# Expert rows added up in DRAM, the last expert's matrices in halves, and a closing norm by 512 columns

## The reference

```
cl = (xf @ w_coarse) + b_coarse                     # 4 groups, the best one is taken
fl_sel = fine logits of that group's 8 experts      # the best two are taken
gate = p_coarse * softmax of the two fine logits
for grp in range(4):                                # 32 experts in all
    hg = silu(xf @ w_gate[grp]) * (xf @ w_up[grp])  # 2048 -> 512, per expert
    hg = hg * gate
    y = y + hg @ w_down[grp]                        # 512 -> 2048
h = h + y
out = rms_norm(h, final_norm)                       # over 2048 columns
```

## Time and profile before

| | before |
|---|---|
| median of three runs | 1869.32 us |
| profiled execution, own time | 1867.9 us |
| span of its records | 1865.8 us |
| matrices of experts 1 to 31: first issue, last bytes | 898.85 us, about 1831 us |
| last up product, last down product end | 1832.75 us, 1841.51 us |
| last VectorE operation ends | 1863.26 us |

### The profile page before, as it was taken

How to read it: one execution, slowest core, us unless ns; L and a number is a source line. 1 busy time by engine, 2 the same in 40 slices (tenths; PEclk the granted TensorE clock), 3 DMA queues, 4 the chain that set the end, 5 groups by cost and what they waited for, 6 DMA issues and landing times.

```text
span 1865.8 us, 36834 instructions
## 1 busy us (share of the span) xinstructions
PE 1666.8 (89%) x16304; PEld 1183.8 (63%) x16304; DVE 446.4 (24%) x1020; ACT 317.4 (17%) x820; POOL 86.0 (5%) x144
## 2 busy tenths in 40 slices
PE   6999999988988999998999888988898888998894
PEld 5888888867777445575876554654556555565552
DVE  2000333588885201014111100111011100101014
ACT  2112222166665101123000000000000000000001
POOL 1000000000000000001000000000000000000000
PEclk9999999999999999998999999999999999999997
DMA  9932344400000935332799999999999999999995
GB/s 319 181 110 91 116 127 169 180 4 4 4 4 4 339 112 203 124 149 95 300 393 427 428 430 425 423 426 434 420 428 422 427 433 413 435 414 434 419 426 235
DMA packets 95237, 509.75 MB, mean 273 GB/s; under 512 B 39324, under 2 KB 43824, under 8 KB 77088
## 3 DMA queue, kind: packets, MB, share of 16 engines
q1 hardware_dynamic: 87080, 490.27, 65.2%
q0 software_dynamic: 7808, 17.28, 3.0%
q10 hardware_dynamic: 248, 0.65, 0.1%
HBM read 497.66 MB, written 23.10 MB: 279 GB/s over the span
## 4 chain that ended last, share of the span: by engine, by line
PE 70%; DMA 20%; DVE 5%; issue 2%; ACT 1%; SPq 0%; DVEq 0%; POOL 0%; ACTq 0%
PE ps L1909 19%; DMA ring<-in_wu 19%; PE ps L1407 15%; PE ps L1732 6%; PE ps L1897 6%; PE ps L1959 6%; PE ps L1750 1%; PE ps L1801 1%; PE ps L1759 1%; PE ps L1818 1%; PE ps L1621 1%; PE ps L1489 1%; PE ps L1448 1%; PE ps L1470 1%; DMA ring<-y_dram 1%
## 5 line engine op out<-in xcount | busy, mean ns | idle before, releaser
L1909 PE MATMUL ps<-ring,rkv 128*64 128x256 f32 x4096 | 473.7, 392 | 67.2 <-DMA ring<-in_wu 45.8
L1909 PEld LDWEIGHTS ps<-ring,rkv 128*64 128x64 f32 x4096 | 337.5, 141 | 211.5 <-DMA ring<-in_wu 54.5
L1407 PE MATMUL ps<-hnT,ring 128*128 128x256 f32 (+1 forms) x1280 | 282.2, 379 | 2.7 <-ACT hnT L471 1.5
L1407 PEld LDWEIGHTS ps<-hnT,ring 128*128 128x128 f32 (+1 forms) x1280 | 239.1, 187 | 48.2 <-issue 10.1
L1959 PE MATMUL ps<-ring,gg 128*64 128x512 f32 x1024 | 238.0, 619 | 32.1 <-issue 16.1
L1959 PEld LDWEIGHTS ps<-ring,gg 128*64 128x64 f32 x1024 | 84.0, 142 | 164.1 <-issue 145.1
L1318 DVE SCALAR_TENSOR_TENSOR gg<-ps,tmp,gg 128x256 f32<-128x256 f32 x32 | 15.4, 483 | 521.3 <-PE ps L1909 521.3
L1897 PE MATMUL ps<-hnT,sw 128*128 (+1 forms) x1024 | 120.5, 279 | 5.0 <-DVE rkv L1293 2.7
L1897 PEld LDWEIGHTS ps<-hnT,sw 128*128 128x128 f32 x1024 | 117.3, 194 | 11.1 <-issue 8.2
L737 ACT ACTIVATE rkv<-ps 128x512 f32<-128x512 f32 x32 | 19.1, 597 | 547.6 <-PE ps L1959 547.6
L1326 DVE COPY rkv<-ps 128x512 f32<-128x512 f32 x31 | 21.4, 691 | 244.0 <-PE ps L1959 244.0
(11 more groups left out here) (352 smaller groups left out, 1597.7 us busy)
## 6 DMA issues: line engine op xcount, KB each, us to landing
ring<-in_wg SPq DMA_DIRECT2D x32, 4096.0 KB, 19.6
ring<-in_wu SPq DMA_DIRECT2D x32, 4096.0 KB, 21.4
ring<-in_wd SPq DMA_DIRECT2D x32, 4096.0 KB, 17.7
ring<-in_w_in SPq DMA_DIRECT2D x7, 4096.0 KB, 15.3
ring<-in_w_out SPq DMA_DIRECT2D x4, 4096.0 KB, 21.3
ring<-in_w_in SPq DMA_DIRECT2D x16, 512.0 KB, 7.5
y_dram<-tmp POOLq DMA_DIRECT2D x1, 4096.0 KB, 21.3
ring<-in_xatt_wk SPq DMA_DIRECT2D x1, 4096.0 KB, 14.1
```

What stands on the lines that cost most here:

```text
L1407: ins = mm(ps[0:rows_, m % 2, 0:T], lhs, hnT[:, k, :], start=k == 0, stop=k == KD - 1)
L1909: ins = mm(ps[CAP * h:CAP * h + CAP, bank, 0:T], xT[:, k, CAP * i:CAP * i + CAP], slot_k(slot)[:, k, T * h:T * h + T], start=k == 0, stop= ...
```

## The change

1. `y_dram` has 2 rows for each token, and the scatter adds to the stored row (`compute_op=ALU.add`). The tensor is no longer zeroed. After the residual is complete (`xw_add`), SyncE stores it there: four DMAs of 512 KB, 2 MB in all (L347), issued behind the down matrix of expert 0. GpSimd waits for them. One more scatter comes first in each pass, and in the first pass all its rows are out of bounds; the last expert's rows are not scattered at the end.
2. The halves of the columns are laid differently: the two halves `n` of the down product are now columns 0 to 1023 and 1024 to 2047, and in `y_dram` and in `tokA` at the end a row holds 512 columns of each.
3. The last expert's up matrix comes in two DMAs (first and second half of the contraction), its down matrix in four of 1 MB (two column halves by two halves of the contraction). TensorE waits for each half by itself.
4. SyncE reads back 2 MB in four DMAs straight into `tokA`, over the residual, as soon as scatter 30 has landed; it waits for no product. The four wide additions on VectorE are gone.
5. The last eight products are ordered by the tuple `FIN`, each with its own increment of `fin_mm`, and VectorE adds them one by one. The table for the square root is loaded on ScalarE ahead of the squares.
6. Semaphores are merged and renamed (`zeroed`, `rel_in`); this moves no instruction.

```diff
-        c[:, TV + b] = 2 * (np.arange(P) + P * b) - BIG
+        c[:, TV + b] = np.arange(P) + P * b - BIG
...
+        def fin_part(b, h, n):
+            o = D // 2 * h + F * n
+            return tokA[:, b, o:o + F]
-        y_dram = nc.dram_tensor("y_dram", (4 * T, D // 2), F32)
+        y_dram = nc.dram_tensor("y_dram", (2 * T, D // 2), F32)
+        FIN = ((0, 0, 0), (0, 0, 1), (0, 1, 0), (1, 0, 0), (1, 0, 1), (0, 1, 1), (1, 1, 0), (1, 1, 1))
+        FIN_BANK = (0, 1, 2, 3, 6, 7, 4, 5)
...
+            def last_expert(j):
+                sp.wait_ge(S["m_gate"], j + 1)
+                weights(S_GATE, "wg", NE - 1)
+                sp.wait_ge(S["m_up"], j + 1)
+                up = a["wu"][NE - 1].rearrange("(p k) n -> p (k n)", p=P)
+                for h, done in ((0, landed[S_UP]), (1, S["up_rest"])):
+                    q = slice(SLOT // 2 * h, SLOT // 2 * h + SLOT // 2)
+                    sp.dma_start(ring[:, S_UP, q], up[:, q]).then_inc(done, 16)
+                sp.wait_ge(S["m_dn"], 2 * j + 1)
+                down = a["wd"][NE - 1].rearrange("(h p c) n -> p h c n", h=2, p=P)
+                for n, h, done in ((0, 0, landed[S_DOWN]), (0, 1, S["dn_lo"]), (1, 0, S["dn_hi"]), (1, 1, S["dn_hi"])):
+                    q = slice(D // 2 * n, D // 2 * n + D // 2)
+                    sp.dma_start(slot_d(S_DOWN)[:, 2 * h:2 * h + 2, q], down[:, h, :, q]).then_inc(done, 16)
...
+            yv = y_dram.ap().rearrange("(b p h) d -> p b h d", p=P, h=2)
+            sp.wait_ge(S["xw_add"], 8)
+            for b in range(TB):
+                hv = tokA[:, b].rearrange("p (n h c) -> p h n c", n=2, h=2)
+                for h in range(2):
+                    sp.dma_start(yv[:, b, h].rearrange("p (n c) -> p n c", n=2), hv[:, h]).then_inc(S["y_init"], 16)
...
-            with sp.Fori(0, NE - 1) as e:
+            with sp.Fori(0, NE - 2) as e:
                 expert(e + 1, e + 1)
+            last_expert(NE - 1)
...
-            sp.wait_ge(S["m_up"], blocks * NE + 1)
+                    last_expert(b * NE + (NE - 1))
             sp.wait_ge(S["rows_out"], blocks * NE)
-            yv = y_dram.ap().rearrange("(b p r h) d -> p b r (h d)", p=P, r=2, h=2)
             for b in range(TB):
-                sp.dma_start(slot_d(S_UP)[:, 2 * b:2 * b + 2, :], yv[:, b]).then_inc(S[f"y_in{b}"], 16)
-            for b in range(TB):
-                sp.wait_ge(S[f"y_in{b}"], 16)
-            sp.sem_inc(S["last_go"], 1)
+                for h in range(2):
+                    sp.dma_start(tokA[:, b, D // 2 * h:D // 2 * h + D // 2], yv[:, b, h]).then_inc(S[f"y_in{b}{h}"], 16)
...
-                if i == 4:
-                    sp.wait_ge(S["rows_out"], blocks * NE + 1)
+                b, h, n = i // 4, i // 2 % 2, i % 2
+                o = D // 2 * n + F * h
                 sp.wait_ge(S["fin_o"], i + 1)
-                sp.dma_start(ov[:, b, q], tokA[:, b, q]).then_inc(S["out_done"], 16)
+                sp.dma_start(ov[:, b, o:o + F], fin_part(b, h, n)).then_inc(S["out_done"], 16)
...
-            pool.wait_ge(S["pool_step"], 1)
-            pool.dma_start(y_dram.ap().rearrange("(p r) (j n) -> p (r j) n", p=P, n=256),
-                           zeros.unsqueeze(1).broadcast_to([P, 32, 256])).then_inc(S["y_zero"], 16)
...
+            pool.memset(tmp[:, 1600 + NE - 1:1600 + NE], 1.0).then_inc(S["pool_step"], 1)
+            pool.wait_ge(S["pool_step"], 1)
+            pool.wait_ge(S["y_init"], 16 * 2 * TB)
+
+            def scatter(e, c):
                 pool.tensor_copy(sidx[:], rows_of[:, ds(e, 1)]).then_inc(S["sidx_ok"], 1)
-                pool.wait_ge(S["sidx_ok"], j + 2)
-                pool.wait_ge(S["m_ya"], j + 2)
-                pool.wait_ge(S["m_yv"], j + 2)
+                pool.wait_ge(S["sidx_ok"], c + 1)
+                pool.wait_ge(S["m_ya"], c + 1)
+                pool.wait_ge(S["m_yv"], c + 1)
                 pool.sem_inc(S["pool_step"], 1)
                 pool.indirect_dma_start(y_dram.ap(), bass.IndirectOffsetOnAxis(sidx[:, 0:1], 0), ysb, None,
-                                        bounds_check=4 * T - 1, oob_is_err=False).then_inc(S["scattered"], 16)
-                pool.wait_ge(S["scattered"], 16 * j + 16)
+                                        bounds_check=2 * T - 1, oob_is_err=False, compute_op=ALU.add).then_inc(S["scattered"], 16)
+                pool.wait_ge(S["scattered"], 16 * c + 16)
                 pool.sem_inc(S["rows_out"], 1)
...
+                scatter(NE - 1, b * NE)
                 pool.wait_ge(S["r_cnt"], 3 * b + 1)
                 pool.sem_inc(S["pool_step"], 1)
-                scatter(0, b * NE)
-                scatter(1, b * NE + 1)
+                scatter(0, b * NE + 1)
+                scatter(1, b * NE + 2)
                 pool.wait_ge(S["r_cnt"], 3 * b + 3)
                 pool.sem_inc(S["pool_step"], 1)
                 with pool.Fori(2, NE - 1) as e:
-                    scatter(e, b * NE + e)
-                pool.wait_ge(S["last_go"], b + 1)
-                pool.sem_inc(S["pool_step"], 1)
-                scatter(NE - 1, b * NE + (NE - 1))
+                    scatter(e, b * NE + e + 1)
...
-                dc.add(V.tensor_scalar(vals[:, b, :, 0], M2[:, b], cst[:, TV + b:TV + b + 1], None, ALU.add))
+                dc.add(V.tensor_copy(vals[:, b, :, 0], cst[:, TV + b:TV + b + 1].broadcast_to([P, NE])))
...
-            for i in range(8):
+            A(warm, warm, ACT.Sqrt)
+            for i, (n, t, h) in enumerate(FIN):
                 act.wait_ge(S["fin_sq"], i + 1)
-                b, q = i // 4, slice(F * (i % 4), F * (i % 4) + F)
-                A(tokB[:, b, q], tokA[:, b, q], ACT.Square, accum_out=sqp[:, i:i + 1]).then_inc(S["sq_done"], 1)
+                A(tokB[:, t, F * (2 * h + n):F * (2 * h + n) + F], fin_part(t, h, n), ACT.Square,
+                  accum_out=sqp[:, 4 * t + 2 * h + n:4 * t + 2 * h + n + 1]).then_inc(S["sq_done"], 1)
...
-            yy = slot_d(S_UP)
-            for b in range(TB):
-                dve.wait_ge(S[f"y_in{b}"], 16)
-                dc.link(V.tensor_tensor(tokA[:, b, :], tokA[:, b, :], yy[:, 2 * b, :], ALU.add))
-                dc.link(V.tensor_tensor(tokA[:, b, :], tokA[:, b, :], yy[:, 2 * b + 1, :], ALU.add))
-            for i in range(8):
-                b, q = i // 4, slice(F * (i % 4), F * (i % 4) + F)
-                dve.wait_ge(S["fin_mm"], i // 4 + 1)
-                V.tensor_tensor(tokA[:, b, q], tokA[:, b, q], ps[:, i, :], ALU.add).then_inc(S["fin_sq"], 1)
+            def last_rows(i):
+                n, t, h = FIN[i]
+                dve.wait_ge(S[f"y_in{t}{h}"], 16)
+                dve.wait_ge(S["fin_mm"], i + 1)
+                V.tensor_tensor(fin_part(t, h, n), fin_part(t, h, n), ps[:, FIN_BANK[i], :], ALU.add).then_inc(S["fin_sq"], 1)
+            def last_var(t, squares):
+                dve.wait_ge(S["sq_done"], squares)
+                dc.link(V.tensor_reduce(stat(5, 0)[:, t:t + 1], sqp[:, 4 * t:4 * t + 4], AX.X, ALU.add))
+                V.tensor_scalar(stat(5, 1)[:, t:t + 1], stat(5, 0)[:, t:t + 1], 1.0 / D, EPS, ALU.mult, ALU.add).then_inc(S["var_done"], 1)
+            def last_out(t):
+                dve.wait_ge(S["std_done"], 6 + t)
+                dc.link(V.reciprocal(stat(5, 2)[:, t:t + 1], stat(5, 2)[:, t:t + 1]))
+                for h in range(2):
+                    for n in range(2):
+                        o = D // 2 * n + F * h
+                        V.scalar_tensor_tensor(fin_part(t, h, n), fin_part(t, h, n), stat(5, 2)[:, t:t + 1], gain_fin[:, o:o + F],
+                                               ALU.mult, ALU.mult).then_inc(S["fin_o"], 1)
+            for i in range(6):
+                last_rows(i)
+            last_var(0, 14 + 5)
+            last_rows(6)
+            last_rows(7)
-            for b in range(TB):
-                dve.wait_ge(S["sq_done"], 18 + 4 * b)
-                dc.link(V.tensor_reduce(stat(5, 0)[:, b:b + 1], sqp[:, 4 * b:4 * b + 4], AX.X, ALU.add))
-                block_rstd(5, b, 6 + b)
-                for i in range(4):
-                    q = slice(F * i, F * i + F)
-                    V.scalar_tensor_tensor(tokA[:, b, q], tokA[:, b, q], stat(5, 2)[:, b:b + 1], gain_fin[:, q], ALU.mult, ALU.mult).then_inc(S["fin_o"], 1)
+            last_out(0)
+            last_var(1, 14 + 8)
+            last_out(1)
...
+                    if rest is not None and k == KD // 2:
+                        pe.wait_ge(S["up_rest"], rest)
...
                     for n in range(2):
+                        if last and n == 0:
+                            pe.wait_ge(S["dn_lo"], 16 * b + 16)
+                        if last and n == 1:
+                            pe.wait_ge(S["dn_hi"], 32 * b + 32)
...
-                                o = D // 2 * h + F * n
+                                o = D // 2 * n + F * h
...
-            pe.wait_ge(S["m_yv"], blocks * NE + 1)
-            for t in range(TB):
-                for n in range(2):
```

(26 more changed lines are left out.)

35 lines of the change are left out of this document (14 added, 21 removed).

## The result

The changed kernel takes 1874.9 us, the median of 20 runs (1870.72 to 1880.82), and the kernel before 1869.07 us, the median of 20 runs. The ratio is 1.0031, with a 95% interval of 1.0024 to 1.0038: it is slower by about 5.8 us. The prediction said 1874 us. It was the difference of two terms, 13.3 us gained in the tail and 18.6 us lost to scatters that add, and the profile after shows both; "tail" stands here for the time from the issue of the last gate matrix to the end of the span.

A forecast was written before the change was run, and what follows sets the result against it. For half of the time the arrival of 31 experts' matrices by DMA bounds the kernel, then a tail. 1867.9 (profiled) - 13.3 + 18.6 = 1873.2 us, 1874 us for the median; range 1857 to 1889 us.

The forecast's parts named there:

- Tail: End of the kernel: matrices in pieces, earlier read-back and no wide additions were to gain 13.3 us.
- Read-back in time: End of the kernel: 2 MB queue behind the down matrix, landing about 1834 to 1838 us, each part before its addition.
- Small edits: Dropped zeros, stored residual, extra empty scatter, column order and matrix pieces: counted as 0; 5 us without cover for the store.
- The adding scatter: Matrix stream: a second read paid like the first, 0.60 us for each of 31 scatters, 18.6 us lost; chance 0.42.
- The price of 0.60 us for a scatter: Matrix stream: extra time per adding scatter, taken between 0.50 and 0.75 us.
- The rule of the Trainium skill on two source reads: Adding scatters: limited by two source reads on one ring, 1.93 times a copy; the term would be 17 us.
- The swizzle rule: Scatters: four neighbouring partitions share one engine; 0.78 us on the fullest engine, 24 us for the term.
- The share of 2.2% or more: Sign of being right: software queue's share of the DMA engines over 940 to 1790 us, in place of 1.2%.
- Hidden reads: Rival on the adding scatters: second read hidden or nearly, 0 to 4 us, kernel 1856 to 1860 us; chance 0.25.
- Half price: Rival on the adding scatters: second read spread evenly or partly hidden, 8 to 12 us, 1864 to 1868 us; chance 0.15.
- Much slower: Rival: adding packets hold their engine to DRAM and back, 40 us, 1896 us; chance 0.12 including a new wait.
- Late landing: Rival: scatters land too late for `ysb`; 20 us landings cost some 30 us; within a shared chance of 0.12.

The follow-up runs named there:

- e2: The changed kernel with scatters that write instead of adding, the sums over a token's two experts left out: 1853.61 us, 0.9938 of the kernel before.
- c1: The changed kernel run again, unchanged: 1874.47 us, 1.0027 of the kernel before.
- e3: The changed kernel with the slots of an expert's tokens spread over the partitions by one constant: 1854.13 us, 0.9941 of the kernel before.
- e4: The kernel before, scatters still writing, with the token slots spread over the partitions: 1859.55 us, 0.9960 of the kernel before.
- e8: The kernel before, scatters still writing, with the token slots packed onto neighbouring partition groups: 1884.34 us, 1.0083 of the kernel before.
- e1: The kernel before with only its scatters made to add to the stored rows: 1887.07 us, 1.0114 of the kernel before.
- e9: The changed kernel, scatters adding, with the token slots packed onto neighbouring partition groups: 1913.16 us, 1.0244 of the kernel before.
- e5: The changed kernel with the last expert's up and down matrices in one DMA each: 1880.12 us, 1.0057 of the kernel before.
- e10: The changed kernel with spread slots and the last expert's up and down matrices in one DMA each: 1857.30 us, 0.9947 of the kernel before.

## Why the prediction was right

**The number.** Both terms were right in kind and somewhat too large: the tail gained 10.6 to 11.4 us for 13.3 us, the stream lost 16.3 to 17.1 us (911.7 and 912.5 us against 895.4 us) for 18.6 us. Their errors cancel, so that the 0.9 us between 1874 us and the median of 1874.9 us is in part luck.

**Tail, 13.3 us predicted.** In e2, where nothing adds, it is 12.8 us. In the changed kernel it is 10.6 us, in its repeat 11.4 us. That the last scatters, which add among the last matrices, take the rest is likely and not shown. The parts: the step from the end of the down product to the end of the span was to shrink from 24.3 to 16.0 us, and is 15.6 us in the changed kernel and in e2. The end of the down product was to come 5.0 us nearer to the end of the last gate product, 20.8 us before; it came 3.6 us nearer in e2 and 1.4 us in the changed kernel (2.8 us in c1). This is the term that was mis-sized: I had the second half of the down matrix landed before its product could begin, and it comes 1.2 to 1.9 us late wherever it is loaded in pieces, except in e3, where the products before it ran slower. In the changed kernel and its repeat the second half of the up matrix is late as well, by 2.1 and 0.7 us. The landing at 1831 us, read from the one trace of the kernel before, was an early one: with the same code at the end the down product waits for its matrix in e4 and e8, by 1.51 and 1.93 us. That the up product would follow the gate product without a stall holds in e2 and for its first half after the change. That it then takes 7.1 us holds there too; in e3 the two together took 15.53 us in place of 14.08 us, at a granted clock of 0.65 in the first 4.4 us, after a stall of 2.63 us ahead of the gate product.

**Read-back in time.** Right: VectorE waits for products only. But its DMAs don't queue behind the down matrix, as I had it. In e2 the last of the down matrix has landed when its product starts at 1831.14 us, and the DMA view from 1831.1 to 1840 us holds only 1.06 MB of the 2.1 MB: the other half had moved before. If it took the engines from the down matrix, that is 2.5 us at 424 GB/s, an estimate; no run holds the read-back up, and in e4 and e8 the matrix is late although the read-back is issued only 2.5 and 3.0 us before it has landed, so the cause of the late half stays open.

**Small edits, 0.** Right as far as can be told: the first gate issue moved within what it does in all kernels, and the 2.3 us by which it is later after the change are there already at the issue of `in_xatt_wk` (671.11 and 673.27 us), long before the residual is stored. The stored residual filled the stretch that was seen idle in the earlier trace rows; windows of the changed kernel, with the columns of that group:

```profile
875.00:880.00 5.00, 2.34 (x10) 2.21 (x10) 3.27 (x21) 0.41 (x2) 0.00 (x0) 0.55 1.03 341
880.00:885.00 5.00, 3.16 (x15) 3.16 (x16) 3.29 (x22) 1.28 (x1) 0.00 (x0) 0.50 0.98 378
885.00:890.00 5.00, 2.90 (x22) 2.71 (x22) 5.00 (x4) 0.00 (x0) 0.26 (x1) 0.93 0.15 58
```

**The adding scatter, 18.6 us predicted.** Right: 20.6 us by e1, 17.5 us between e2 and the changed kernel, and 17.1 us in the stream before the last gate issue. A row of 4 KB holds its engine for 0.327 us in place of 0.159 us, as it would if a second read were paid like the first. The price of 0.60 us for a scatter was a choice between 0.50 us of lost time and 0.75 us of the lone one, and it came out near the fullest engine's: four rows of 0.159 us are 0.64 us. The rule of the Trainium skill on two source reads ("Collectives: The Full Stack", section on the bandwidth ceiling, 1.93 times) agrees in size; here a row takes 2.06 times as long. The swizzle rule gave 24 us with a price for a row worked out from the mean, 0.19 us, that was too high: it holds the small packets too. With 0.168 us more for a row it gives 20.8 us. That the fullest engine counts and not the mean is what e3, e4, e8 and e9 show; on spread slots the sum of rows times price is too large (the last row of the table above). The share of 2.2% or more is 2.3%, and the last gate issue is 19.4 us later, where 18 us were written.

**Rivals.** Hidden reads: refuted by e1. Half price, the mean over the engines: refuted by e3 and e8, which change the time and leave the mean. Much slower: only lone adding packets show such waits (0.5 to 1.1 us); among the matrices of e1 the longest row takes 0.53 us. Late landing: 12.7 us where 17.7 us would do; right that it does not bind.

What stays open, beside the late half of the down matrix and the cost of adding on spread slots: why the profiled stream of e5 is 5 us longer than those of the changed kernel, with no edit in it; its runs range from 1873.45 to 1884.75 us.

## What to carry to other kernels

When a stream of DMAs is the bound, look at what a side transfer takes on the fullest of the 16 engines, and not only at its bytes or its share of the mean: here the same rows at the same share made the adding kernel 45 us slower or 12 us faster than the kernel before, by the partitions on which they stood. Spreading the used slots by one constant made both kernels faster, by 6.9 us and 16.8 us, and turned the slower change into one that is 12 us faster than before. An addition moved into a transfer was not free here: a row held its engine twice as long. It is worth it only where that time is not on the bound, or costs less than what it removes.

## What the runs showed of the hardware

- An adding indirect DMA of 4 KB rows holds a DMA engine 0.327 us for a row among other transfers (e1, the changed kernel), a writing one 0.159 us (before, e2). With no other transfer the first eight adding rows took 0.5 to 1.1 us (e1).
- Which partitions hold a scatter's rows changes the time at an unchanged share of the DMA engines: measured each against the kernel before on its chip, packed and spread slots are 23.2 us apart when writing (e8, e4) and 57.4 us when adding (e9, e3).
- GpSimd's own time for the instruction rose from 0.97 us to 1.57 us (medians), and the time to landing in the stream from 11.8 us to 12.7 us.
- A scatter all of whose rows are out of bounds lands after 2.8 us and moves nothing that can be seen in the stream.
- After a stall of 3.0 to 3.5 us the last up product took 8.6 to 8.8 us in before, e1, e5 and e10, at a granted clock of 0.61 to 0.66 in its first 4.3 to 4.5 us, a mix of the two levels of 1.2 and 2.4 GHz. In e4 and e8, after stalls of 3.07 and 3.37 us, the granted clock stayed at 1.00 and it took 7.13 us. So such a stall lowers the clock in some executions and not in others.
